# Rounding h and the weights into two parts for the q/k/v projections, convolving out of PSUM, and taking the inverse norms from token-wise sums

## What is computed

```python
h_lat = _modulate(_rms_norm(x, norm1[i]), m_lat[0], m_lat[1])
p_lat = jnp.split((h_lat @ w_in).astype(jnp.float32), idx, axis=-1)
...
def _conv1d_centred(x, w):
    l = x.shape[1]
    xp = jnp.pad(x, ((0, 0), (1, 1), (0, 0)))
    return xp[:, :l] * w[0] + xp[:, 1:l + 1] * w[1] + xp[:, 2:] * w[2]

def _l2norm(t):
    return t * lax.rsqrt(jnp.sum(t * t, axis=-1, keepdims=True) + 1e-6)

qkv = jax.nn.silu(_conv1d_centred(jnp.concatenate([q, k, v], axis=-1), conv_w))
q = _l2norm(_heads(q, GDN_HEADS)) * (GDN_DK ** -0.5)
k = _l2norm(_heads(k, GDN_HEADS))
```

## Time and profile before

| what | value |
| --- | --- |
| median of 3 runs | 1615.28 us (1615.0 to 1617.74) |
| the profiled execution's own time | 1616.57 us |
| its span | 1614.8 us |
| PE busy | 1572.9 us, 97% |
| DVE, ACT, POOL busy | 79%, 37%, 31% |
| first stage | from 0 to about 277.5 us |

### The profile page before, as it was taken

The page is one execution under the profiler, slowest core; times in us unless marked ns, Lnnn a source line. Parts: engine busy times, 40 slices in busy tenths (PEclk is TensorE's granted clock), DMA queues, the critical chain, the costliest instruction groups (busy, mean ns, idle before and its releaser), DMA issues.

```text
span 1614.8 us, 20799 instructions
## 1 busy us (share of the span) xinstructions
PE 1572.9 (97%) x8010; PEld 1171.0 (73%) x8010; DVE 1273.6 (79%) x1861; ACT 589.8 (37%) x984; POOL 495.5 (31%) x483
## 2 busy tenths in 40 slices
PE   7999999999999989999999999999999999999997
PEld 2455554987489966565578888888888888788886
DVE  5488878499866678888787389889889888967658
ACT  2544333553243312323464432222222222344455
POOL 5001101121143345656313633433434433600001
PEclk9999999999999989999999999999999999999999
DMA  9276553865398740100433246444352511233365
GB/s 348 74 254 215 179 188 127 255 174 128 93 271 252 210 170 14 27 14 26 148 128 108 88 124 124 124 95 139 75 141 78 119 53 29 88 133 97 101 147 169
DMA packets 216031, 214.99 MB, mean 133 GB/s; under 512 B 41221, under 2 KB 156239, under 8 KB 215708
## 3 DMA queue, kind: packets, MB, share of 16 engines
q1 hardware_dynamic: 200144, 183.97, 36.7%
q0 software_dynamic: 9392, 26.48, 7.5%
q10 hardware_dynamic: 6396, 3.20, 0.7%
HBM read 171.50 MB, written 65.19 MB: 147 GB/s over the span
## 4 chain that ended last, share of the span: by engine, by line
PE 55%; DVE 6%; issue 1%; ACT 1%; POOL 1%; DMA 0%; ACTq 0%; DVEq 0%; POOLq 0%
PE PS L2257 10%; PE PS L2255 10%; PE PS L2259 10%; PE PS L2113 4%; PE PS L2292 4%; PE PS L2294 4%; PE PS L2293 4%; PE PS L2128 3%; DVE Qbd L2587 2%; PE PS L2215 1%; PE PS L2217 1%; PE PS L2216 1%; PE PS L2150 1%; DVE AT L2603 1%; DVE Ex L2568 0%
## 5 line engine op out<-in xcount | busy, mean ns | idle before, releaser
L2758 DVE SCALAR_TENSOR_TENSOR acc<-PS,fcol,acc 128x945 f32<-128x945 f32 (+2 forms) x176 | 215.1, 1222 | 29.2 <-ACT acc L2380 23.7
L2758 DVE SCALAR_TENSOR_TENSOR act<-PS,fcol,act 128x945 f32<-128x945 f32 (+2 forms) x176 | 215.1, 1222 | 21.6 <-ACT act L2380 16.2
L2255 PE MATMUL PS<-h2hi,whi 128*128 128x512 f32 x704 | 219.5, 389 | 0.0
L2259 PE MATMUL PS<-h2hi,wlo 128*128 128x512 f32 x704 | 219.4, 389 | 0.0
L2257 PE MATMUL PS<-h2lo,whi 128*128 128x512 f32 x704 | 219.3, 389 | 0.0
L2024 POOL TENSOR_TENSOR wlo<-wu,whi 128x1024 fp32r<-128x1024 f32 x44 | 106.4, 2423 | 214.1 <-ACT whi L2373 214.0
L425 PE MATMUL PS<-hT,wq 128*128 128x512 f32 (+1 forms) x432 | 163.1, 537 | 0.0
L2259 PEld LDWEIGHTS PS<-h2hi,wlo 128*128 128x128 f32 x704 | 132.1, 188 | 27.5
L2257 PEld LDWEIGHTS PS<-h2lo,whi 128*128 128x128 f32 x704 | 132.1, 188 | 27.4
L2255 PEld LDWEIGHTS PS<-h2hi,whi 128*128 128x128 f32 x704 | 132.1, 188 | 27.4
L425 PEld LDWEIGHTS PS<-hT,wq 128*128 128x128 f32 x432 | 81.6, 190 | 78.4 <-issue 75.6
(11 more groups left out here) (336 smaller groups left out, 2981.0 us busy)
## 6 DMA issues: line engine op xcount, KB each, us to landing
wm<-in_w_mod_dram SPq DMA_DIRECT2D x24, 1024.0 KB, 7.6
wu<-in_w_up_dram SPq DMA_DIRECT2D x44, 512.0 KB, 3.9
t_sums<-in_w_down_dram POOLq DMA_DIRECT2D x12, 1024.0 KB, 9.9
raw<-t_sums SPq DMA_DIRECT2D x44, 256.0 KB, 2.6
raw<-in_w_down_dram SPq DMA_DIRECT2D x33, 256.0 KB, 2.7
wq<-in_w_in_dram SPq DMA_DIRECT2D x12, 512.0 KB, 8.9
gdn_x_image<-ztile SPq DMA_DIRECT2D x10, 516.0 KB, 9.9
gdn_xt_image<-ztile SPq DMA_DIRECT2D x10, 516.0 KB, 8.0
```

Source lines behind the costliest of these rows:

```text
L2255: pe.matmul(PS[:, b + half, :], whi[k][u][:, kk, :], h2hi[:, 4 * half:4 * half + 4, kk, :], start=(kk == 0), stop=False)
L2259: mm = pe.matmul(PS[:, b + half, :], wlo[k][u][:, kk, :], h2hi[:, 4 * half:4 * half + 4, kk, :], start=False, stop=(kk == KT - 1))
L2758: tp = v.scalar_tensor_tensor(out=t_[:, r0:r1, c0:c1], in0=up[:, r0 + dr:r1 + dr, c0 + dc:c1 + dc], scalar=tap_col(j, k, f), in1=t_[:, r0: ...
```

## The change

h is no longer kept in float32. Each tile of h is first made in one of three buffers `hs`, stored from there to memory (`h_out`), and rounded by ACT to `hhi`; what the rounding left goes to `hlo`, by DVE for the first four tiles and by POOL for the other six. The weights are split in the same way: ACT rounds (`w_high`), POOL subtracts (`w_low`). Each float32 matmul becomes three in the rounded format (`three`): high by high, high by low, low by high. The same is done to the 48 columns.

The middle tap is now the scale of ACT's copy out of PSUM (`centre`), and DVE's two others read the PSUM banks, which so stay in use longer. The sums of squares are now made per token: `csq` is the loaded operand and one column of ones the moving one, so a norm is one number on each partition. ACT takes the root of 8 or 10 columns, DVE inverts them (`inverse`), PE turns them to rows inside a later product (`turn_norms`), DVE copies the rows to SBUF (`norm_row`), POOL stores them to memory, waits, and reads them back to all partitions (`spread`), and DVE multiplies (`unit`). v goes to memory within the stage (`v_out`, on ACT's queue), and the second stage loads `hT` again, in ten tiles, before its PE work.

Core of the diff:

```diff
+                def w_low(kind, h):
+                    g.wait_ge(s_wqh[kind], h + 1)
+                    g.tensor_tensor(wqlo[kind][:, :, :], wq[kind][:, :, :], wqhi[kind][:, :, :], ALU.subtract).then_inc(s_wql[kind], 1)
...
+                def spread(kind, h):
+                    n = NT if kind else NL
+                    g.wait_ge(s_bank[kind], h + 2)
+                    g.dma_start(r_dram[kind, h, 0:n, :], nrow[kind][0:n, :]).then_inc(s_nrs[kind], 16)
+                    g.wait_ge(s_nrs[kind], 16 * (h + 1))
+                    if kind:
+                        g.wait_ge(s_un[0], h + 1)
+                    elif h:
+                        g.wait_ge(s_un[1], h)
+                    g.dma_start(crn[:, 0:n * P], r_dram[kind, h, 0:n, :].rearrange("t p -> (t p)").rearrange("(o n) -> o n", o=1)
+                                .to_broadcast([P, n * P])).then_inc(s_nrb[kind], 16)
...
                 for h in range(H):
...
+                    if h:
+                        spread(1, h - 1)
+                    if h + 1 < H:
+                        w_low(0, h + 1)
+                        w_low(1, h + 1)
+                    spread(0, h)
...
+                    if h + 1 < H:
+                        w_low(2, h + 1)
+                spread(1, H - 1)
...
+                def three(out, kind, k, t0, n):
+                    hi, lo = wqhi[kind][:, k, :], wqlo[kind][:, k, :]
+                    pe.matmul(out, hi, hhi[:, k, t0:t0 + n], start=(k == 0), stop=False, skip_group_check=True)
+                    pe.matmul(out, hi, hlo[:, k, t0:t0 + n], start=False, stop=False, skip_group_check=True)
+                    return pe.matmul(out, lo, hhi[:, k, t0:t0 + n], start=False, stop=(k == KT - 1), skip_group_check=True)
+
+                def product(kind, h, between=None):
+                    pe.wait_ge(s_wql[kind], h + 1)
...
                     for b, (t0, n) in enumerate(PARTS[kind]):
+                        if kind == 1 and b == 2:
+                            pe.wait_ge(s_bank[1], h + 1)
                         for k in range(KT):
...
+                            mm = three(PS[:, BANK[kind] + b, 0:n], kind, k, t0, n)
+                        if b == 0 and between is not None:
+                            turn_norms(*between)
                     mm.then_inc(s_mm[kind], 1)
...
+                    for t in range(NT if kind else NL):
+                        mm = pe.matmul(PS[:, norm_bank(kind), t:t + 1], csq[:, tile_cols(t)], ones[:, 0:1], start=True, stop=True)
...
+                def turn_norms(kind, h):
+                    n = NT if kind else NL
+                    pe.wait_ge(s_nri[kind], h + 1)
+                    pe.transpose(PS[0:n, norm_bank(kind), 256:256 + P], nri[kind][:, 0:n], ident[:, :]).then_inc(s_ntr[kind], 1)
...
+                def head(h):
+                    product(0, h, (1, h - 1))
+                    turn_v(h - 1)
                     product(1, h)
                     sums(0, h)
+                    product(2, h, (0, h))
                     sums(1, h)
```

On DVE, head h is now this list (`parts(a, b)` are `part` a to b-1, each now two steps of 512 columns):

```diff
+                def head(h):
+                    parts(8 * h, 8 * h + 2)
+                    if h:
+                        norm_row(1, h - 1)
                     conv(0, h)
+                    if h:
+                        copy_v(h - 1)
+                    parts(8 * h + 2, 8 * h + 4)
+                    if h:
+                        unit(1, h - 1)
                     conv(1, h)
+                    inverse(0, h)
+                    parts(8 * h + 4, 8 * h + 6)
+                    norm_row(0, h)
+                    parts(8 * h + 6, 8 * h + 8)
                     unit(0, h)
                     conv(2, h)
+                    inverse(1, h)
```

On the SP queue the ten `h_out` come ahead of everything else that the heads need, and `load(kind, h + 1)` stands among the `rest`:

```diff
+                for h in range(H):
+                    for m, i in enumerate(range(8 * h + 2, min(8 * h + 10, MPARTS))):
+                        if m == 2:
+                            load(0, h + 1)
+                        if m == 5:
+                            load(1, h + 1)
                         rest(i)
+                        if i % 4 == 2 and i > 4:
+                            sums_out(i // 4 - 1)
+                        if i > 5 and n < 20:
+                            zeros(n)
+                            n += 1
+                    load(2, h + 1)
...
+                for t in range(NT):
+                    sp.dma_start(hT[:, :, tile_cols(t)], hT_dram[t]).then_inc(s_h2[t], 16)
```

More of the change, by code:

```diff
@@ L316, in _ @@
+                sums_out(7)
+                sp.wait_ge(s_msp, 16 * 8)
+                sp.dma_start(wgA[:, :, :], win[:, :, GV0:GV0 + P]).then_inc(s_wg0, 16)
+                for i in range(3):
+                    sp.wait_ge(s_hst[i], 16 * len(range(i, NT, 3)))
+                sp.wait_ge(s_vst, 16 * H)
                 sp.wait_ge(s_zi, 320)
@@ L536, in _ @@
                 x_stats(1, 2, 4)
+                w_high(0, 0)
                 a.wait_ge(s_gain, 1)
-                for t in range(4):
-                    h_tile(t)
+                h_tile(0)
+                for t in range(1, 4):
+                    if t < 3:
+                        h_tile(t)
+                        h_high(t - 1)
+                    else:
+                        h_high(t - 1)
+                        h_tile(t)
+                h_high(3)
                 x_stats(2, 4, NL)
+                w_high(1, 0)
@@ L736, in _ @@
+                for h in range(H):
+                    head(h)
+                norm_row(1, H - 1)
                 copy_v(H - 1)
+                unit(1, H - 1)
                 v.wait_ge(s_hb, 32)
@@ L2106, in gate_part @@
                         if n == 0:
[L2107 removed]
+                            pe.wait_ge(s_hr[2 * half], 64)
                         if n or half:
```

434 lines of the change are left out of this document (241 added, 193 removed).

## The result

The changed kernel takes 1656.54 us (median of 4 runs, 1652.95 to 1658.68), the kernel before 1616.51 beside it: a ratio of 1.0245, 95% interval 1.022 to 1.027. The profiled execution has a span of 1656.6 us at a mean granted clock of 0.965, against 1614.8 and 0.988. PE is busy for 1562.7 us of it (94%), DVE 1222.2 (74%): PE works less than before, and the time grows.

What follows compares the result with a forecast made beforehand. PE, never waiting in the heads, was taken as the bound, then a 33.5 us chain against its 23.1 us of work. Stage 1 +33.7 and second stage +4.3, about +38 on the median 1615.3, gave 1653, range 1630 to 1677.

Steps and rivals of the forecast that it cites:

- The likeliest case: Heads: period longer than before by the chain of two transfers and k weights; 1653, own range 1640 to 1668; chance 0.62.
- PE's own work: Heads and 48 columns: cheaper matmuls -41 us, sums and turns +7; a head of PE work becomes 43.6 us.
- The chain: Heads, from product(1, h)'s end through load, low weights, q's trip and DVE to turn_norms(1, h): 33.5 us against PE's 23.1.
- The rule on transfers: POOL's store and read: 2.0 us plus bytes over 436 GB/s, so 2.0 and 3.2; forecast took 3 and 5.5.
- The waits: PE in the q product, ahead of the turn of k's norms: about 10.4 us, three times, and about 4 at the tail.
- The clock: Behind PE's waits the granted clock falls to 0.50: 1.7 us for each of five waits, +8.5.
- Stage 1, by its pieces: First stage: +8.4 to product(1, 0), +13.4 to product(1, 1), +5 periods, -1.6 tail, +8.5 clock; +33.7 in all.
- periods: Heads, from one end of product(1) to the next: 53.8 us against 51.3 before; two more periods, +5.
- tail: From the last product(1) to the first stage's end: 37.2 us against 38.8 before, -1.6.
- The second stage: the step that failed: Second stage: hT must be loaded before PE's first work, +3.1, and gate rows queue behind it; +4.3, bounds 3 and 8.
- largely under PE's own delay: Second stage: 7 us more of queue ahead of the gate rows was taken to be largely hidden by PE's delay.

Runs made afterwards that it cites:

- POOL's order: Changed kernel with POOL issuing spread(0, h), the trip of q's inverse norms, ahead of w_low(1, h+1): 1629.8 us, ratio 1.0081.
- all seven: Profiles sharing this second stage: the changed kernel and six runs editing only its first stage; keys(2) stands 32.7 to 33.9 us behind the stage's start.
- Three experiments: Gate rows on ACT's queue (1651.29 us); plus keys(0), keys(1) first on PE (1651.34); six h tiles ahead of the rows, atop three combined changes (1624.21).
- the start: Changed kernel with tiles 8 and 9's statistics and turns earlier, and conv(0, 0) ahead of DVE's parts: 1648.7 us, ratio 1.0198.
- the second stage: Changed kernel with gate rows' store and six loads on ACT's queue: 1651.29 us; with keys(0), keys(1) and one V slice ahead of gate sums: 1651.34.
- 34.7 together: Changed kernel with POOL's spread moved up, the earlier first-stage statistics, and the second stage's queue and order edits: 1621.79 us, ratio 1.0038.
- more cover for the waiting engine: Changed kernel with PE turning k's norms behind the second slice of the next q product instead of the first: 1646.55 us, ratio 1.0186.

## Why the prediction came out as it did

The forecast was 1653, the measured median 1656.5. The likeliest case is the one that happened, and its mechanism is shown by the run with POOL's order: the change of one place in one list takes 26.7 of the 40 us away.

- **PE's own work.** The sums came as taken: the ten columns of k, in 20 records, take 2.29 us (row at 177.60), 0.11 a record. From one centre copy to the next, 147.17 to 162.06, it is 14.9 us for turn and k product; taken were 1.1 + 13.6.
- **The chain.** 32.8 us in head 1 against 33.2. Part by part: to the issue of the load 7.6 (8.3 taken), landing 6.9 (6), high and low 3.4 (3.5), store 3.3 (4), read 7.0 (6.5), the rest 4.7 (4.9). No term is off by more than 1.
- **The rule on transfers.** The fit of the Trainium skill (DMA: Bandwidth & Descriptors, Anatomy of one DMA — SWDGE (gpsimd) path) gave an estimate of 2.0 and 3.2 us; the trace disagrees for the large one, which took 3.8 us at the least and 8.1 at most, and agrees for the small one only at times. The view of DMA issues from 100 to 310 us in the changed kernel (count, KB each, median us to landing):

```profile
crn<-inverse_norms POOLq DMA_DIRECT2D x4, 640.0 KB, 4.2
crn<-inverse_norms POOLq DMA_DIRECT2D x4, 512.0 KB, 6.5
inverse_norms<-nrow POOLq DMA_DIRECT2D x4, 4.0 KB, 2.5
inverse_norms<-nrow POOLq DMA_DIRECT2D x4, 5.0 KB, 4.3
```

  More bytes land sooner here, so size is not what sets it. What goes with it is how busy the 16 DMA engines are. From the store of a row to the issue of its read, and the DMA share in just that stretch:

  | run | stores | DMA share | us |
  | --- | --- | --- | --- |
  | changed kernel | at 123.94, 235.42, 294.25 | 0.02 to 0.07 | 1.9 to 2.2 |
  | changed kernel | at 179.92, 253.25 | 0.52, 0.54 | 3.3, 3.1 |
  | changed kernel | at 279.64 | 0.75 | 4.5 |
  | changed kernel | at 143.80, 199.79 | 0.97, 1.00 | 6.2, 6.1 |
  | POOL's order | at 269.24 | 0.02 | 1.9 |
  | POOL's order | at 231.18, 255.16 | 0.56, 0.75 | 2.8, 4.5 |
  | POOL's order | five, at 114.43 to 209.33 | 0.95 to 1.07 | 6.0 to 6.5 |

  All sixteen stores fall on one line, whether they carry 4 or 5 KB. So the trace meets the estimate of 2.0 us where the engines are idle, and takes three times as long where they are full.
- **The waits.** 7.8, 9.4, 5.9 and 1.3 us, not three of 10.4 and one of 4. (In head 0 the prediction's own times, 124.9 and 137.6, make it 12.7. The turn came at 138.9, 1.3 late, but PE was at it only at 131.1, 6.2 late: the sums started 1.4 late, and the clock was at 0.50 from 102 to 110 and again at 124. The wait paid for this slow work.) From the end of the k product to the turn it is 32.8, 31.0 and 22.0 us in heads 1 to 3, and PE had 23.4, 25.0 and 20.7 us of work in it (the turn's start, less the wait, less the product's end). So head 1 is as forecast (33.5 against 23.1); in head 2 the chain is 2 us shorter and PE's work 2 longer, since 4 us of it, from 236, are at the lower clock; the last head has no weights left to load, which shortens the chain by 11 and not by 6.
- **The clock.** 2.5, 1.8 and 2.4 us behind three waits instead of 1.7 each. Mis-sized, by a third. The prediction read its price off a gap "of 277.1 to 279.5"; in the timeline of before PE works again from 278.73, and was idle for 1.7 us only, so a short gap was enough there. And it gave the clock five places; in the changed kernel it was at 0.50 in more, from 74 to 79, at 93 to 97, 124 and 236, of which the last two cost nothing, as shown above.
- **Stage 1, by its pieces.** To the end of `product(1, 0)` 95.8 (92.1 predicted), to that of `product(1, 1)` 162.1 (157.9, without the clock), periods of 55.3 and 54.0 (53.8, without it), tail 34.9 (37.2). In all +29.7 to the second stage's start against +33.7: without the clock the predicted pieces were 3.6 us short together, and the 8.5 for the clock, which the measured pieces already hold, was too much.
- **The second stage: the step that failed.** It was taken as +4.3 with bounds of 3 and 8, since 7 us of queue would lie "largely under PE's own delay". It is 12 in this profile, 9.3 to 10.5 at `keys(2)` in all seven, outside both. The first use of a gate row is 10.0 late, by the rows of the stage: the rows themselves 4.5 (323.89 - 308.43 = 15.5 us behind the start, 289.64 - 278.69 = 11.0 before), since PE does three slices of V ahead of the gate sums, and these wait for h (their first matmul stands 4.2 us behind the stage's start instead of 0.8, the +3.4 that the prediction had as +3.1, and they run 1.1 longer); the issue behind the reloads 2.2; from the store to the first load 3.3; the load itself 0. PE was not delayed so long that it could hide this: it waits 5.7 us at `keys(2)`. What fails is the sentence that let the queue lie under PE. Three experiments show the parts, and no run got back more than 4.4 us at `keys(2)`; PE needs the same h whose bytes are in the way.

The two errors, 4 us too much and 8 too little (5 by the middle of the seven profiles), partly cancel. That the forecast is within 3.5 us of the median is in part luck; the sum is better than its terms.

What stays open: POOL's order, the start and the second stage bring 26.7, 7.8 and some 3 to 5 us alone, 37 to 40 in all, and 34.7 together; the start's part halves, and waits for inverse norms come back, but which chain is then the longest was not settled. Nor what makes the clock fall behind some of the one-column sums and not behind others: no run changes them alone. That busy DMA engines make the small stores land late is read from sixteen of them; no run changes the traffic by itself.

## What to carry to other kernels

Cheaper work on the bounding engine is worth its price only as long as every other chain fits under what is left of it: add the longest chain across the engines up, transfers included, before the work is cheapened. In a list that several chains share, what is ready must not stand behind what waits; here one line moved in POOL's list was worth 27 us, while more cover for the waiting engine brought 10 and moved the rest of the wait on. And whatever is spilled in one stage is reloaded in the next ahead of something small and urgent: here the bytes in front of it counted more than the queue that it was in.
